# Opening of a hybrid decoder step: activation table, split of the first weight unit, and TensorE's waits

## What is computed

```python
def rmsnorm(x, g):
    y = x * lax.rsqrt(jnp.mean(x * x, axis=-1, keepdims=True) + EPS)
    return y * g

def chunk_gmlp(x, norm_g, w_in, b_in, sgu_g, w_s, b_s, w_out, b_out):
    h = rmsnorm(x, norm_g)
    z = jax.nn.gelu(h @ w_in + b_in)             # (tokens, 4096)
    u, v = z[..., :D_GATE], z[..., D_GATE:]      # D_GATE = 2048
    v = rmsnorm(v, sgu_g)
    mix = einsum('gij,bnjgc->bnigc', tril(w_s), v in chunks of 128) + b_s
    return (u * mix) @ w_out + b_out, v
```

## Time and profile before

| | |
|---|---|
| median of 3 runs | 1825.77 us (1823.91 to 1826.25) |
| profiled execution | 1823.55 us |
| its span in the trace | 1821.9 us |
| PE busy | 1730.2 us, 95% |
| DVE busy | 1278.5 us, 70% |
| ACT busy | 970.7 us, 53% |
| mean granted clock of PE | 0.983 of full |

### The profile page before, as it was taken

The page is one execution under the profiler, slowest core; times in us unless marked ns, Lnnn a source line. Parts: engine busy times, 40 slices in busy tenths (PEclk is TensorE's granted clock), DMA queues, the critical chain, the costliest instruction groups (busy, mean ns, idle before and its releaser), DMA issues.

```text
span 1821.9 us, 25052 instructions
## 1 busy us (share of the span) xinstructions
PE 1730.2 (95%) x8926; PEld 1442.5 (79%) x8926; DVE 1278.5 (70%) x1696; ACT 970.7 (53%) x1211; POOL 74.5 (4%) x141
## 2 busy tenths in 40 slices
PE   6999999999988899999996999999999999999997
PEld 5698989999865767777775888888888888888885
DVE  5467365553378575556538889898898989898995
ACT  4344243332344454444333667676867677676763
POOL 0000000000001102211100000000000000000000
PEclk8999999999999999999997999999999999999998
DMA  8342433334322101100014889898989989888982
GB/s 303 116 150 73 159 117 139 139 138 145 110 102 76 30 0 44 44 29 29 29 59 162 311 335 361 326 374 303 374 327 342 349 332 352 334 353 324 381 321 109
DMA packets 71469, 368.91 MB, mean 202 GB/s; under 512 B 8240, under 2 KB 18752, under 8 KB 34336
## 3 DMA queue, kind: packets, MB, share of 16 engines
q1 hardware_dynamic: 64256, 351.82, 51.5%
q0 software_dynamic: 5408, 11.43, 2.1%
q10 hardware_dynamic: 1728, 4.63, 0.7%
HBM read 365.61 MB, written 2.24 MB: 202 GB/s over the span
## 4 chain that ended last, share of the span: by engine, by line
PE 80%; DVE 11%; issue 4%; ACT 4%; DMA 1%; DVEq 0%; ACTq 0%; SPq 0%; PEldq 0%
PE bank L1538 24%; PE bank L1540 23%; PE bank L1539 23%; PE bank L1821 2%; PE bank L1975 1%; PE bank L1957 1%; ACT at_r L812 1%; PE bank L1983 1%; DVE sks L1227 1%; ACT at L772 1%; PE bank L1741 1%; PE bank L1630 1%; DVE rs_t L927 1%; DVE rs_t L928 1%; DVE at_r L1402 0%
## 5 line engine op out<-in xcount | busy, mean ns | idle before, releaser
L1538 PE MATMUL bank<-at_r,at_r 128*128 128x512 f32 (+3 forms) x2076 | 760.2, 366 | 26.9 <-PE bank L1540 9.2
L1540 PE MATMUL bank<-at_r,at_r 128*128 128x512 f32 (+3 forms) x2076 | 747.2, 360 | 0.0
L1539 PE MATMUL bank<-at_r,at_r 128*128 128x512 f32 (+3 forms) x2076 | 746.6, 360 | 0.0
L1306 DVE TENSOR_TENSOR at_r<-at,at_r 128x2048 fp32r<-128x2048 f32 x264 | 597.0, 2289 | 73.1 <-ACT at_r L812 69.1
L812 ACT ACTIVATE at_r<-at 128x2048 fp32r<-128x2048 f32 x264 | 496.2, 1913 | 1.6 <-PE bank L1540 1.6
L1538 PEld LDWEIGHTS bank<-at_r,at_r 128*128 128x128 f32 (+1 forms) x2076 | 387.3, 187 | 88.9 <-issue 16.9
L1540 PEld LDWEIGHTS bank<-at_r,at_r 128*128 128x128 f32 (+1 forms) x2076 | 387.2, 187 | 55.0
L1539 PEld LDWEIGHTS bank<-at_r,at_r 128*128 128x128 f32 (+1 forms) x2076 | 387.9, 187 | 50.3
L938 DVE TENSOR_TENSOR at_r<-at,at_r 128x2048 fp32r<-128x2048 f32 x57 | 130.4, 2289 | 103.6 <-ACT at_r L569 103.5
L569 ACT ACTIVATE at_r<-at 128x2048 fp32r<-128x2048 f32 x57 | 108.9, 1913 | 132.3 <-PE bank L1540 92.9
L1227 DVE TENSOR_REDUCE sks<-at 128x8 f32<-128x1024 f32 x64 | 77.9, 1216 | 79.0 <-ACT at L772 79.0
(11 more groups left out here) (314 smaller groups left out, 1450.3 us busy)
## 6 DMA issues: line engine op xcount, KB each, us to landing
at<-in_m_un SPq DMA_DIRECT2D x264, 1024.0 KB, 4.8
at<-in_d_gu SPq DMA_DIRECT2D x22, 1024.0 KB, 4.9
at<-in_w_in SPq DMA_DIRECT2D x16, 1024.0 KB, 6.0
at<-in_d_down SPq DMA_DIRECT2D x11, 1024.0 KB, 5.0
at<-in_w_out SPq DMA_DIRECT2D x8, 1024.0 KB, 5.0
at<-in_c_lat POOLq DMA_DIRECT2D x64, 128.0 KB, 2.3
at<-in_w_o SPq DMA_DIRECT2D x2, 2048.0 KB, 10.1
at<-in_w_uq SPq DMA_DIRECT2D x2, 1152.0 KB, 10.6
```

The costliest lines, as they stand in the source:

```text
L1306: TT(low_part[raw_slot[q]], raw[raw_slot[q]], high_part[hi_slot[q]].bitcast(f32), SUB).then_inc(u_lo, 1)
L1538: mm(out, xh, wh, start=first, stop=False)
L1539: mm(out, xh, wl, start=False, stop=False)
L1540: return mm(out, xl, wh, start=False, stop=last)
```

## The change

1. ScalarE begins with a Gelu of one element, written to a scratch word (`rs_t`) that nobody reads before it is written again. The table with Gelu is so loaded once, ahead of the columns.
2. ScalarE splits unit 0 before it scales the columns, and scales the eight columns in one row.
3. VectorE makes unit 0's low part in four quarters of 512 elements, each ahead of the low column of the same block; only residual column 0 stands among them. Residual columns 1 to 3 follow, then low columns 4 to 7, unit 1's low part, residual columns 4 to 7. The counter of `in_order` is handed in so that unit 0 is counted as done.
4. TensorE doesn't wait for `u_lo` 1. For the first tile it waits before each block k for `n_lo` k + 1; for the later tiles of the first eight it waits for `n_lo` o + 1, at most 8.

```diff
-        def in_order(step):
-
-            done = [0]
+        def in_order(step, done=None):
+
+            done = [0] if done is None else done
...
             act.wait_ge(s_zero, 1)
             act.wait_ge(s_const, 32)
+            A(rs_t[0:1, 0:1], G[0:1, 0:1], ACT.Gelu_apprx_tanh)
+            ahead(0)
             for k in range(KC):
                 act.wait_ge(ntr, k + 1)
                 A(hTp[0][:, k, :], bank[k][:, 0:NTOK], ACT.Copy, scale=G[:, G_A + k:G_A + k + 1]).then_inc(n_hi, 1)
-                if k == 3:
-                    ahead(0)
             load_gmlp_rows()
...
-            ahead = in_order(dense_low)
+            first_unit = [0]
+            ahead = in_order(dense_low, first_unit)
...
-            for half in range(2):
-                ks = range(4 * half, 4 * half + 4)
-                for k in ks:
-                    columns_low(k, bank[k][:, 0:NTOK])
-                for k in ks:
-                    TS(xT[:, k, :], bank[k][:, 0:NTOK], G[:, G_BO + k:G_BO + k + 1], None, ADD).then_inc(x_new, 1)
-                ahead(half)
+            def keep(k):
+                TS(xT[:, k, :], bank[k][:, 0:NTOK], G[:, G_BO + k:G_BO + k + 1], None, ADD).then_inc(x_new, 1)
+
+            dve.wait_ge(u_hi, 1)
+            for k in range(4):
+                c = slice(512 * k, 512 * k + 512)
+                i = TT(low_part[0][:, c], raw[0][:, c], dense_high_part[0][:, c].bitcast(f32), SUB)
+                if k == 3:
+                    i.then_inc(u_lo, 1)
+                columns_low(k, bank[k][:, 0:NTOK])
+                if k == 0:
+                    keep(0)
+            first_unit[0] = 1
+            for k in range(1, 4):
+                keep(k)
+            for k in range(4, 8):
+                columns_low(k, bank[k][:, 0:NTOK])
+            ahead(1)
+            for k in range(4, 8):
+                keep(k)
...
-            def dense_unit(n, chunks):
-
-                pe.wait_ge(u_lo, n + 1)
+            def dense_unit(n, chunks, first=False):
+
+                if not first:
+                    pe.wait_ge(u_lo, n + 1)
...
-                    w = dense_unit(2 * n + h, 4)
+                    w = dense_unit(2 * n + h, 4, first=n == 0 and h == 0)
...
-                            pe.wait_ge(n_lo, max(4, o + 1))
+                            pe.wait_ge(n_lo, min(8, o + 1))
                             pe.wait_ge(x_new, o + 1)
                         elif n == 0:
                             pe.wait_ge(n_lo, 8)
                         for k in range(4):
+                            if o == 0 and h == 0:
+                                pe.wait_ge(n_lo, k + 1)
```

## The result

| | kernel before | changed kernel |
|---|---|---|
| median of 8 runs each | 1824.16 us (1822.13 to 1826.25) | 1817.71 us (1814.83 to 1821.05) |
| ratio | | 0.9965, 95% interval 0.9954 to 0.9977 |
| profiled execution (span) | 1823.55 us (1821.9) | 1817.68 us (1815.9) |
| first product / unit 1's first product | 19.84 / 30.56 | 14.09 / 25.12 |

The change is worth 6.4 us (4.2 to 8.4 by the interval), against 6.0 forecast.

A forecast was written before the change was run, and what follows sets the result against it. TensorE, busy 95% of the span, was taken as the bound, so an earlier start carries through. First product 5.8 us earlier, unit 1 at 24.6 instead of 30.56: 1825.8 - 6.0 = 1819.8 us, range 1818.0 to 1823.0.

The forecast's parts named there:

- The base of the sum: Whole kernel: the median before, 1825.8 us, from which 6.0 was subtracted to give 1819.8.
- Size of the gain: Whole kernel: unit 1's first product starts 6.0 us earlier, carried whole to the end; own range 5.0 to 6.5.
- Table: ScalarE's opening: the table load runs 7.3 to 8.6 under unit 0's transfer, taking 1.28 us off the path.
- High part first, quarters, one residual column: Opening on ScalarE and VectorE: reordered, split work brings the first product to 14.02 from 19.84, 5.8 us earlier.
- The clock: TensorE's opening: half clock from near 14.8 until a rise at 19.2, putting unit 1 at 24.6.
- The forecast case: TensorE's opening: idle 1.8 us, granted clock falls near 14.8, later rises, unit 1 at 24.6; chance 0.73.
- its ends of 24.1 and 25.0: Unit 1's first product: 24.1 if the clock rises at 18.2, 25.0 if at 20.2.
- What is late next: VectorE after the opening: low parts of units 2 to 4 by 33.2, first evacuation then; nothing takes the gain back.
- The clock does not fall: Rival, TensorE's opening: full rate throughout, unit 1 at 23.4, gain 7.1 us, 1818.6; chance 0.10.
- The clock stays low: Rival, TensorE's opening: rise only at 24.95, unit 1 at 27.2, gain 3.3 us, 1822.5; chance 0.06.
- Absorption: Rival, behind the first projection: a stage not tied to TensorE leaves less than half the gain, 1823 to 1826; chance 0.06.
- Code placement: Rival, expert passes: shifted instructions add one 1.77 us pause in each of seven, 12.4 us, 1832.2; chance of slower 0.05.

The follow-up runs named there:

- two later jobs: The changed kernel measured again, unaltered, twice against the kernel before: ratios 0.9975 and 0.9961.
- The second profile: The changed kernel run again, with nothing altered: median 1818.17 us, ratio 0.9975 to the kernel before.
- third profile: The changed kernel run once more, with nothing altered: median 1817.17 us, ratio 0.9961 to the kernel before.
- gap kernel: The changed kernel plus 8 idle transposes on TensorE just ahead of the first product: 1813.56 us (0.9947), repeated 1816.69 us (0.9955).

## Why the prediction was right or wrong

**The base of the sum: wrong, and it decided.** This is the step that failed: the term 1825.8 in "on the median 1825.8 - 6.0 = 1819.8" takes the median of three runs for the kernel's. Eight runs gave 1824.16, and in the later jobs 31, 22 and 11 runs gave 1823.50, 1823.86 and 1824.32. With 1824.16 the same sum reads 1818.2, 0.5 above the measured 1817.71, and the range of 1818.0 to 1823.0, moved down by the same 1.6 us, begins at 1816.4 and holds it. The profiled execution was the better base: 1823.55 - 6.0 = 1817.5 stood in the text, and the measured profile is at 1817.68. Three runs over a spread of 2.3 us should have moved the lower end of the range by one more microsecond, the more so as two of the three lay within half a microsecond of the top.

**Size of the gain: right, with some luck.** 6.0 forecast (5.0 to 6.5 as its own range), 6.4 measured, 4.6 and 7.1 by the ratios of the two later jobs. In the first profile the shift is 5.4 us at unit 1, below the forecast's own 5.5 to 6.4, and another 0.5 comes behind it, less than three profiles of the changed kernel differ by there (1790.8 to 1792.1). So the 6.4 is not shown to be the change's alone.

**Table: right.** Load at 7.15 ("near 7.3"), none near 33, 1.28 us off the path under cover of the transfer, bare again when it is taken back (1.3 us without the later landing). The one-element Gelu took 0.20 us against 0.3. The rule of the Trainium skill that a switch costs a drain besides ("ScalarE: Activation LUTs", "What ACT_TABLE_LOAD costs") is not seen at the first load of any of the traces: 0.02 us at most stand between load and ACTIVATE.

**High part first, quarters, one residual column: right.** High part at 10.32 (10.41 forecast), quarter 0 at 12.38 (12.38), first product 14.09 (14.02), the quarters 0.69 us long and 1.06 us from block to block, the reciprocal roots at 24.32 (24.4). The second profile had everything 0.3 later with a later landing, as the range allowed.

**The clock: the rate right, the reason wrong in this profile.** I expected a fall near 14.8 and a rise at 19.2; the rate changed at 19.8. But nothing fell. By the spacing of the products the array was at its lower clock from the first on, and it had not risen during the transposes (4.69 us against 4.20 before); the record does not show it. That the rate changed near the forecast's 19.2 all the same is luck. Unit 1 came at 25.12 instead of 24.6: the first three products were slow already, so block 1 began at 15.51 instead of 15.08 (0.4 of the 0.5 us), and ten instead of 9.65 of the other 33 ran at half rate. The forecast case is real (third profile, 24.37), and its ends of 24.1 and 25.0 were too narrow for one kernel's executions: 24.4 to 25.6 seen.

**What is late next: right in effect, wrong on unit 4.** I let ScalarE split unit 4 as soon as unit 0 was free, and put the first evacuation at 33.2. Unit 4 had not landed:

```profile
30.43 1.91 ACT L569 ACTIVATE at_r<-at 128x2048 fp32r<-128x2048 f32 x1 [5.84 <-DMA at<-in_w_in]
35.36 0.63 ACT L598 ACTIVATE at<-at 128x512 f32<-128x512 f32 x1 [3.02 <-DVE at L1026]
```

The first evacuation started at 34.58 against 34.98 before, so all but 0.4 of the 5.4 us is lost on that engine. TensorE did not care, as argued: up to 86 us it waited for no other engine behind its first product, and unit 2 started at 33.89, 5.3 us earlier than before. The slack, not the sum, carried this step. On ScalarE's side the landing of unit 4 is now what a still earlier start would meet.

**Rivals.** "The clock does not fall" gave 7.1 us; none of the three profiles of the changed kernel showed it, the gap kernel made it true (unit 1 at 23.5 to 23.7 against 23.4 worked out). "The clock stays low" to 24.95 was not seen. Absorption was not seen: 1791.3 and 1790.8 from unit 1 to the end. Code placement: no sign of it; seven extra pauses of 1.77 us would add 12.4 us to the second column of the table, whose thirteen values differ by 6.0.

## What to carry to other kernels

Where the first product waits for a chain of small steps on two other engines, order them by what that product reads, cut the big step to the product's grain, and give the consumer a wait per piece: here taking any one of the last two back cost 1.6 to 3.2 us of the first product's 5.8, the wait per piece most. A function table loads for nothing under the first transfer, but only if something asks for it there; alone it was worth 1.2 us in the trace and nothing that the times could tell. Before a forecast of a few microseconds on a kernel of this length, count how much half-clock time the profile holds and lay the sum on the profiled execution or on many runs; a median of three moved by 1.6 us.

## What the runs showed of the hardware

- The record of the granted clock can read 1.00 at the start of an execution while the array runs at half rate: 13 products at 0.43 us stood in a stretch recorded at 1.00, and 24 transposes took 4.6 to 4.7 us there, against 2.57 behind 6 us of idle work. In these traces the record has no entry before the first rise (at 19.9 us in the changed kernel's first profile, at 11.3 in the kernel before), and the stretches read 1.00 until then. The spacing of equal matmuls tells the clock, the record alone does not. The slow start agrees with the Trainium skill, "TensorE: Matmul & The Clock Gate", section "What's actually happening", by which the throttled state is the default.
- With eight idle transposes (1.1 to 1.6 us) in the gap ahead of the first product, the products behind them ran at full rate in all three profiles.
- Behind a gap of 1.97 us the clock fell in some executions (the gap kernel's second profile) and not in others (its first), with the same work around it.
- The first table load of each trace was followed by its ACTIVATE within 0.02 us, whether it had waited for the gain columns, for the transposes or for unit 0. Loads further on stand ahead of waits for other engines (1.72 us ahead of the first Gelu before) and can't show it.
